# One block per layer from the output projection to the first expert gathers, with the first token tile ahead of the second

## The chip, the cores and the metric

One NeuronCore of a Trainium2 chip runs the whole program. The metric is the device time of one execution in microseconds (us), as the median of several runs. The engines of the core are PE (TensorE, matrix products; PEld is its loading of weights), DVE (VectorE), ACT (ScalarE), POOL (GpSimd) and SP (SyncE, which issues most DMAs). SBUF is the working memory, PSUM takes what PE computes.

## What is computed

Two layers of a network over 256 context and 512 latent tokens, 1024 numbers each, everything in 32-bit floats. Each layer is an attention part and a part with experts. What matters here is the end of the one and the start of the other:

```python
x = x + gate1 * (o @ w_out)                                  # output projection, gated
h = modulate(rmsnorm(x, norm2), shift, scale)                # normed, (1 + scale), + shift
q = (h @ wq).reshape(T, P_HEADS, 2, P_DKEY // 2)             # 16 half heads of 128
s = jnp.einsum("thpd,hpnd->thpn", q, sub_keys)               # scores against 128 keys each
sv, si = lax.top_k(s, P_TOPK)                                # 16 best of 128
cand = (sv[:, :, 0, :, None] + sv[:, :, 1, None, :]).reshape(T, P_HEADS, P_TOPK * P_TOPK)
fv, fi = lax.top_k(cand, P_TOPK)                             # 16 best of 256, per head
...                                                          # eidx from si and fi, gate = softmax(fv)
a = gelu(einsum("tkd,td->tk", u_tab[eidx], h)) * gate        # 128 experts for each token
x = x + gate2 * einsum("tk,tkd->td", a, v_tab[eidx])
```

The rows `u_tab[eidx]` and `v_tab[eidx]` lie in HBM side by side and are fetched by an indirect DMA, one row of 8 KB for each token and expert.

## The kernel before, in words

Tokens are cut into tiles of 128 (P): tiles 0 and 1 are the context, 2 to 5 the latent tokens. A `Stage` holds buffers and semaphores. A `Block` is a set of programs, one for each engine, with a barrier of all engines at its end; the semaphores of a stage are cleared by SP behind it. One block follows another.

In each layer two tiles are brought as far as their scores before the gathers start (tiles 0 and 1 in layer 0, tiles 2 and 3 in layer 1), and the others follow beside the gathers. Five blocks lie one behind another:

1. `turn_h` (L334): PE transposes the two tiles of attention output, ACT copies them to `m.hT`. SP issues the loads for this block and the next: the output weights in two halves of 2048 KB (L376), the gate rows and the norm's vectors. In layer 1 only columns 512 to 1023 are turned, the others lie in `m.hT` already.
2. `project` (L387): PE multiplies, chunk of 512 columns by chunk and tile by tile (L418, 64 matmul instructions in four groups of 16); DVE multiplies by the gate (L450) and POOL adds to `m.R` (L461).
3. `modulated_norm` (L272): ACT squares and sums both tiles (L294) and takes one root (L296), DVE scales and shifts (L317, L320), PE transposes (L329), ACT copies to `m.hT` (L300). SP prefetches four chunks of `p_wqk` (L1708) and stores one row of the scale.
4. `first_scores` (L1715): `p_wqk` holds for each of 16 half heads one chunk of 576 KB, its query weights and its keys. They pass through a ring of four (`pre_w`). For each, PE multiplies the chunk with both tiles at once (L1746, 256 columns), ACT copies the queries (L1771), PE multiplies them with the keys (L1755), ACT copies the scores (L1775). Chunk h is loaded when the scores of chunk h-4 are done. Behind every fourth half head DVE runs `top16` for the first tile (MAX8, FIND_INDEX8, MATCH_REPLACE8, twice) over the scores, adds up the pairs (L1792) and runs `top16` over those. The second tile's scores go to DRAM (L1736).
5. `run_experts` (L2542): 128 slots for each tile. In slot n POOL issues the gather of expert n of 128 tokens into a ring of eight (L2637, 1024 KB), DVE takes the dot product with `h` (L2734), ACT applies gelu and the gate and makes a diagonal (L2754, L2756, L2760), PE adds the weighted rows into PSUM (L2771). Before the first slot, DVE runs `choose(0, True)`, which makes the expert numbers and the gates of the first tile (L2653 to L2703), and POOL waits for it:

```python
                    if n == 0:
                        pool.wait_ge(chosen, t + 1)
```

SP's queue in this block begins with the constant `iota`, the loads of the work beside the gathers (`beside.begin`: three chunks of 512 KB of output weights and rows of 512 KB), the gate `g`, and the scores of the second tile back from DRAM (L2601, four loads of 256 KB). `choose(t)` for the next tile is spread over the slots by `ChoicePlan`. `beside` is other work on PE, ACT and DVE, laid out by slot numbers by hand: in layer 0 the attention and the scores of tiles 2 to 5 (`LatentMixer`, `NextFront`), in layer 1 those of tiles 4 and 5 (`LatentPair`).

An fp32 matmul of the program is two MATMUL instructions on PE in the profile; a transpose is one.

## Time and profile before

| | |
|---|---|
| median of 3 runs | 4538.05 us (4537.26 to 4540.35) |
| span of the profiled execution | 4536.7 us |
| median of the runs less this span | 1.35 us |
| DMA moved | 1564.87 MB, mean 345 GB/s |
| busy: PE, DVE, ACT, POOL | 83%, 57%, 38%, 38% |
| first gather issued, layer 0 and layer 1 | 555.57 and 3166.40 us |
| gathers | 1280, of 1024 KB |

The profile is of one execution. Its own time outside the span is not given apart; the runs' median lies 1.35 us above the span, and this is taken as what lies around it. Times in the rows are microseconds from the start of the span. A timeline row is start, duration, engine, line, operation, what it wrote and read, how many instructions are merged in it, and in brackets how long the engine was idle before and what ended that. Granted clock 1.00 is 2.4 GHz and 0.50 is 1.2 GHz; a window's value is a mean over both.

### The profile page before, as it was taken

The numbers are of one execution on the slowest core, as the hardware profiler recorded it, in microseconds if no ns is written. First come the engines' busy times: TensorE is split into PE (matmuls) and PEld (weight loads), VectorE is DVE, ScalarE is ACT, GpSimd is POOL, SyncE is SP. The second block draws the span as 40 slices with busy tenths as digits, with TensorE's granted clock in tenths as the row PEclk, the third lists the DMA queues.
The fourth block names the chain that finished last, engine by engine and source line by source line (L and its number), as shares of the span: only waits on it lengthen the run. The fifth ranks groups of instructions, "written<-read, shape, count | busy, mean of one in ns | idle before, by whom it ended". The sixth has DMA issues, their size and how long they took to land. (4 is left out here: it accounts for less than half of the span.)

```text
span 4536.7 us, 43969 instructions
## 1 busy us (share of the span) xinstructions
PE 3771.8 (83%) x12422; PEld 1913.6 (42%) x12422; DVE 2602.3 (57%) x5662; ACT 1740.7 (38%) x5087; POOL 1715.4 (38%) x1358
## 2 busy tenths in 40 slices
PE   6987688899899898888889967675989997877777
PEld 2443544554455454444444423545444452222222
DVE  3533587656856856755654433335775557666544
ACT  1112155444544544433333322421664433333333
POOL 0100044434434444444444422000433534556675
PEclk9988899999999999999999988798999999999999
DMA  4363499999999999999999971014999999999998
GB/s 169 113 237 147 154 420 401 420 420 420 407 420 420 410 420 419 419 420 421 418 417 420 421 310 54 4 61 150 402 377 396 422 422 416 413 421 421 419 421 357
DMA packets 251863, 1564.87 MB, mean 345 GB/s; under 512 B 30946, under 2 KB 45186, under 8 KB 80228
## 3 DMA queue, kind: packets, MB, share of 16 engines
q0 software_dynamic: 185088, 1342.36, 71.7%
q1 hardware_dynamic: 64596, 216.23, 12.5%
q10 hardware_dynamic: 1936, 3.48, 0.2%
q8 instruction: 99, 1.62, 0.1%
q14 instruction: 144, 1.18, 0.1%
HBM read 1551.50 MB, written 10.46 MB: 344 GB/s over the span
## 5 line engine op out<-in xcount | busy, mean ns | idle before, releaser
L2771 PE MATMUL ps<-ex_ring,ex_diag 128*128 128x512 f32 x5120 | 2493.9, 621 | 506.1 <-ACT ex_diag L2760 481.6
L2637 POOL DMA_INDIRECT ex_ring<-in_p_uv,ex_expert x1280 | 1650.1, 1289 | 2014.0 <-PE ps L2771 1523.6
L2734 DVE SCALAR_TENSOR_TENSOR ex_ring<-ex_ring,H 128x1024 f32<-128x1024 f32 x1280 | 1561.7, 1225 | 1170.4 <-DMA ex_ring<-in_p_uv,ex_expert 1156.0
L2771 PEld LDWEIGHTS ps<-ex_ring,ex_diag 128*128 128x128 f32 x5120 | 924.6, 194 | 1728.9 <-ACT ex_diag L2760 916.5
L2754 ACT ACTIVATE ex_act_w<-ex_dots 128x1 f32<-128x1 f32 x1280 | 258.6, 202 | 1519.6 <-DVE ex_ring L2734 1512.6
L2760 ACT ACTIVATE ex_diag<-ident_sb,ex_weight 128x128 f32<-128x128 f32 x1280 | 514.6, 402 | 92.2 <-issue 5.4
L2756 ACT ACTIVATE ex_weight<-ex_act_w,ex_gates 128x1 f32<-128x1 f32 x1280 | 377.9, 295 | 90.6 <-issue 3.1
L685 PE MATMUL ps<-win_w,hT 128*128 128x512 f32 (+1 forms) x480 | 191.9, 557 | 1.9 <-PEq L281 1.4
L1917 PEld LDWEIGHTS ps<-bs_hT,bs_w 128*128 128x128 f32 x1024 | 127.4, 196 | 33.9 <-issue 33.9
L685 PEld LDWEIGHTS ps<-win_w,hT 128*128 128x128 f32 x480 | 90.3, 191 | 106.0 <-issue 103.8
L1917 PE MATMUL ps<-bs_hT,bs_w 128*128 128x128 f32 x1024 | 127.0, 278 | 0.3 <-issue 0.3
L1746 PE MATMUL ps<-hT,pre_w 128*128 128x256 f32 x512 | 115.6, 379 | 2.7 <-PEq L281 2.7
L461 POOL TENSOR_TENSOR R<-R,pout_tmp 128x512 f32<-128x512 f32 x8 | 10.1, 1265 | 267.6 <-DVEq L452 267.6
L2754 ACT ACT_TABLE_LOAD x72 | 92.4, 1283 | 47.1 <-DVE ex_ring L2734 45.9
L2734 DVE DVE_READ_ACCUMULATOR ex_ring<-ex_ring,H 128x1 f32 x1280 | 105.9, 83 | 0.0
L1746 PEld LDWEIGHTS ps<-hT,pre_w 128*128 128x128 f32 x512 | 95.0, 190 | 15.0 <-issue 3.3
L700 ACT ACTIVATE ph_sq<-ps 128x512 f32<-128x512 f32 (+1 forms) x24 | 12.4, 517 | 160.6 <-PE ps L685 160.6
L901 PEld LDWEIGHTS ps<-KV,bs_probsT 128*128 128x128 f32 x480 | 62.9, 192 | 24.0 <-issue 24.0
L418 PE MATMUL ps<-wout_w,hT 128*128 128x512 f32 x128 | 61.7, 644 | 13.5 <-DMA wout_w<-in_o_w_out 7.3
L2042 PEld LDWEIGHTS ps<-bs_w,bs_hT 128*128 128x128 f32 x512 | 63.4, 195 | 15.8 <-issue 15.8
L730 DVE TENSOR_REDUCE ph_ss<-ph_sq 128x8 f32<-128x512 f32 (+1 forms) x24 | 14.1, 586 | 96.2 <-ACT ph_sq L700 96.2
L1917 PE MATMUL ps<-K,bs_w 128*128 128x256 f32 x256 | 66.3, 382 | 0.0
(396 smaller groups left out, 3221.6 us busy)
## 6 DMA issues: line engine op xcount, KB each, us to landing
bs_w<-in_p_wqk SPq DMA_DIRECT2D x80, 576.0 KB
ca_mod_w<-in_w_mod SPq DMA_DIRECT2D x24, 1024.0 KB, 9.1
ex_ring<-in_p_uv,ex_expert POOLq DMA_INDIRECT x1280, 14.7
pre_w<-in_p_wqk SPq DMA_DIRECT2D x32, 576.0 KB, 3.7
win_mod_w<-in_w_mod SPq DMA_DIRECT2D x16, 1024.0 KB, 4.8
bs_w<-in_e_w_out_tiles SPq DMA_DIRECT2D x32, 512.0 KB
win_w<-in_e_w_in SPq DMA_DIRECT2D x9, 1024.0 KB, 11.3
mod_mod_w<-in_w_mod SPq DMA_DIRECT2D x8, 1024.0 KB, 13.1
```

The lines of the kernel that those rows point to most:

```text
L418: mm = pe.matmul(m.ps[:, b, 0:chunk], m.hT[:, k, (t - m.h0) * P:(t - m.h0 + 1) * P], w[:, q, k, :], start=(k == 0), stop=(k == KC - 1))
L685: mm = pe.matmul(m.ps[:, u % 4, 0:halves * 256], m.hT[:, k, t * P:(t + 1) * P], pre.w[:, n % 2, 0:halves, k, :], start=(k == 0), stop=(k = ...
L901: mm = pe.matmul(self.O[:, cols], self.probsT[:, r % 2, x * P:(x + 1) * P], KV[:, self.blocks(n)[j], vals], start=(j == 0), stop=(j == las ...
L1746: mm = pe.matmul(m.ps[:, h % 2, 0:NTL * P], pre.w[:, h % RING, k * P:(k + 1) * P], m.hT[:, k, cols], start=(k == 0), stop=(k == KC - 1))
L1917: mm = pe.matmul(m.ps[:, self.q_banks[u % nq], 0:cols], w[:, j * P:(j + 1) * P], self.turned_of(self.tiles_of(u), j), start=(j == 0), stop ...
L2042: mm = pe.matmul(m.ps[:, 7, c % 4 * P:(c % 4 + 1) * P], self.hT[:, k, :], w[:, k * P:(k + 1) * P], start=(k == 0), stop=(k == KC - 1), ski ...
L2637: pool.indirect_dma_start(ring[:, r, :], None, uv_rows, bass.IndirectOffsetOnAxis(ap=expert[:, t % 2, n:n + 1], axis=0),).then_inc(landed[ ...
L2734: dve.scalar_tensor_tensor(out=ring[:, r, 0:D], in0=ring[:, r, 0:D], scalar=1.0, in1=h_of(t + t0), op0=ALU.mult, op1=ALU.mult, accum_out=d ...
L2754: act.activation(act_w[:, b:b + 1], dots[:, t % 2, n:n + 1], ACT.Gelu)
L2756: act.activation(weight[:, b:b + 1], act_w[:, b:b + 1], ACT.Copy, scale=gates[:, t % 2, n:n + 1])
L2760: act.activation(diag[:, b, :], m.ident[:, :], ACT.Copy, scale=weight[:, b:b + 1]).then_inc(diag_ready, 1)
L2771: mm = pe.matmul(mix_banks(t)[:, half, :], diag[:, b, :], ring[:, r, D + half * BANK:D + (half + 1) * BANK], start=(n == 0), stop=(n == SL ...
```

## The change

The blocks 1 to 4 of each layer and `choose(0, True)` become one block, `first_choice`. Its second argument of tiles is the same pair, but the first tile goes ahead: PE turns both, projects the first (all columns), then the second, turns the first tile's norm, computes its 16 half heads with 128 columns each, and then the second tile's. Unit u is half head u % 16 of tile u // 16. The second tile's norm is turned behind unit 8. So every chunk of `p_wqk` is loaded twice, 32 loads in place of 16. Output weights come in eight loads of 512 KB, each with a semaphore. The gate's product and sum are both on DVE, POOL has no part. DVE norms the first tile before it takes the second's sums, and behind the choice it runs `expert_numbers`, the code of `choose(0, True)` as a function; ACT's exp for it stands behind unit 26. The second tile's scores stay in SBUF, in `m.later_scores` (`m.Qc`, whose life is longer now, or rows 0 and 1 of `m.R`), where `run_experts` reads them: no store and no loads through DRAM. In `run_experts` POOL's first gather has no semaphore to wait for, and counts of `chosen`, `exped`, `weighed` and `sc_read` are lower by one. `LatentPair` gets buffers of its own for what lay in `m.R`. `modulated_norm`, still used elsewhere, squares into the place of its result instead of a scratch buffer.

```diff
--- before.py
+++ after.py
...
-                    act.activation(sq[:, :], m.R[:, t, :], ACT.Square, accum_out=ss[:, t:t + 1])
+                    act.activation(h_of(t), m.R[:, t, :], ACT.Square, accum_out=ss[:, t:t + 1])
...
+def expert_numbers(dve, m, layer, t, best, pos, at_, iota, hot, posf, part, partf, num, shift, total, shifted, chosen, exped, weighed):
...
+    dve.drain()
+    dve.sem_inc(shifted, 1)
+    dve.tensor_copy(partf, part)
+    dve.drain()
+    halves = posf.rearrange("p (h s) k -> p h s k", s=2)
+    h4 = hot.rearrange("p (h k) i -> p h k i", k=TOPK)
+    for half in range(2):
+        dve.tensor_tensor(hot, iota.unsqueeze(1).broadcast_to([P, SLOTS, TOPK]),
+                          partf[:, half, :].unsqueeze(2).broadcast_to([P, SLOTS, TOPK]), ALU.is_equal)
+        dve.drain()
+        dve.tensor_tensor(h4, h4, halves[:, :, half, :].unsqueeze(2).broadcast_to([P, PH, TOPK, TOPK]), ALU.mult)
+        dve.drain()
+        dve.tensor_reduce(num[:, half, :], hot, AX.X, ALU.add)
+        dve.drain()
+    dve.scalar_tensor_tensor(out=num[:, 0, :], in0=num[:, 0, :], scalar=float(NK), in1=num[:, 1, :], op0=ALU.mult, op1=ALU.add)
+    dve.drain()
+    dve.tensor_scalar(m.expert[:, t % 2, :], num[:, 0, :], float(layer * NK * NK), None, ALU.add)
+    dve.wait_ge(exped, 1)
...
+    dve.tensor_tensor(m.gates[:, t % 2, :].rearrange("p (h k) -> p h k", k=TOPK), shift,
+                      total.unsqueeze(2).broadcast_to([P, PH, TOPK]), ALU.mult)
...
+def first_choice(nc, m, a, layer, tiles, stream, w_out, first, src_of, h_of):
...
+    NU = 2 * NH
+    HTURN, EXP_AT = 8, 26
...
+        o_loaded, q_loaded = s.sems("o_loaded", KC), s.sems("q_loaded", RING)
...
+        def load_q(sp, u):
+            sp.dma_start(w_q[:, u % RING, :], a["p_wqk"][layer, u % NH]).then_inc(q_loaded[u % RING], 16)
...
+                for k in range(KC):
+                    sp.dma_start(w_o[:, k, :], w_out[k * P:(k + 1) * P, :]).then_inc(o_loaded[k], 16)
+                sp.dma_start(gate[:, :], rows(mods[stream:stream + 1, 2 * D:3 * D])).then_inc(gate_loaded, 16)
+                sp.dma_start(gain[:, :], rows(a["norm2"][layer:layer + 1, :])).then_inc(vec_loaded, 16)
+                sp.dma_start(scale[:, :], rows(mods[stream:stream + 1, 4 * D:5 * D])).then_inc(vec_loaded, 16)
+                sp.dma_start(shift_row[:, :], rows(mods[stream:stream + 1, 3 * D:4 * D])).then_inc(vec_loaded, 16)
+                if stream:
+                    sp.dma_start(other[:, :], mods[0:1, 4 * D:5 * D]).then_inc(vec_loaded, 16)
+                for u in range(RING):
+                    load_q(sp, u)
+                sp.dma_start(iota[:, :], rows(a["iota"])).then_inc(iota_loaded, 16)
+                sp.wait_ge(scale_ready, 1)
+                sp.dma_start(keep, (other if stream else scale)[0:1, :]).then_inc(kept, 16)
+                for u in range(RING, NU):
+                    sp.wait_ge(scored, u - RING + 1)
+                    load_q(sp, u)
+                sp.wait_ge(kept, 16)
...
+                def turn(n):
+                    for k in range(first, KC):
+                        tr = pe.transpose(m.ps[:, 2 * n + k // 4, (k % 4) * P:(k % 4 + 1) * P],
+                                          src_of(tiles[n])[:, k * P:(k + 1) * P], m.ident[:, :])
+                    tr.then_inc(o_turned, 1)
+                def out(n):
+                    order = [(k, h) for k in range(KC) for h in range(2)] if n == 0 else [(k, h) for h in range(2) for k in range(KC)]
+                    for k, h in order:
+                        if n == 0 and h == 0:
+                            pe.wait_ge(o_loaded[k], 16)
+                            if k == first:
+                                pe.wait_ge(o_copied, 1)
+                        if n == 1 and h == 0 and k == first:
+                            pe.wait_ge(o_copied, 2)
+                        mm = pe.matmul(m.ps[:, 4 + 2 * n + h, :], m.hT[:, k, cols(n)], w_o[:, k, h * BANK:(h + 1) * BANK],
+                                       start=(k == 0), stop=(k == KC - 1))
+                        if k == KC - 1:
+                            mm.then_inc(out_done, 1)
...
+                def query(u):
+                    pe.wait_ge(q_loaded[u % RING], 16 * (u // RING + 1))
+                    if u % NH == 0:
+                        pe.wait_ge(h_copied, u // NH + 1)
+                    if u >= 2:
+                        pe.wait_ge(qT_ready, u - 1)
+                    for k in range(KC):
+                        mm = pe.matmul(m.ps[:, 4 + u % 2, 0:P], w_q[:, u % RING, k * P:(k + 1) * P], m.hT[:, k, cols(u // NH)],
                                        start=(k == 0), stop=(k == KC - 1))
                     mm.then_inc(q_done, 1)
...
+                def score(u):
+                    pe.wait_ge(qT_ready, u + 1)
+                    if u < 2:
+                        pe.wait_ge(out_taken, 3)
+                    else:
+                        pe.wait_ge(taken, u - 1)
+                    pe.matmul(m.ps[:, 6 + u % 2, 0:P], qT[:, u % 2, :], w_q[:, u % RING, KC * P:(KC + 1) * P],
+                              start=True, stop=True).then_inc(scored, 1)
+                for n in range(2):
+                    turn(n)
+                for n in range(2):
+                    out(n)
+                hturn(0)
+                for u in range(NU):
+                    query(u)
+                    if u:
+                        score(u - 1)
+                    if u == HTURN:
+                        hturn(1)
+                score(NU - 1)
...
+                def copy_turned(n, sem, copied, k0):
+                    act.wait_ge(sem, n + 1)
+                    act.copy(m.hT[:, k0:KC, cols(n)],
+                             m.ps[:, 2 * n + k0 // 4:2 * n + KC // 4, :].rearrange("p b (k c) -> p (b k) c", c=P)).then_inc(copied, 1)
+                def root(n):
+                    act.wait_ge(out_taken, (1, 3)[n])
+                    act.activation(sq[:, :], m.R[:, tiles[n], :], ACT.Square, accum_out=ss[:, n:n + 1])
+                    act.drain()
+                    act.activation(ss[:, n:n + 1], ss[:, n:n + 1], ACT.Sqrt, bias=m.eps[:, :], scale=1.0 / D).then_inc(rooted, 1)
+                def query(u):
+                    act.wait_ge(q_done, u + 1)
+                    if u >= 2:
+                        act.wait_ge(scored, u - 1)
+                    act.copy(qT[:, u % 2, :], m.ps[:, 4 + u % 2, 0:P]).then_inc(qT_ready, 1)
+                def score(u):
+                    act.wait_ge(scored, u + 1)
+                    dst = sc if u < NH else later
+                    act.copy(dst[:, u % NH, :], m.ps[:, 6 + u % 2, 0:P]).then_inc(taken, 1)
+                for n in range(2):
+                    copy_turned(n, o_turned, o_copied, first)
+                root(0)
+                copy_turned(0, h_turned, h_copied, 0)
+                root(1)
+                for u in range(NU):
+                    query(u)
+                    if u:
+                        score(u - 1)
+                    if u == HTURN:
+                        copy_turned(1, h_turned, h_copied, 0)
+                    if u == EXP_AT:
+                        act.wait_ge(shifted, 1)
+                        act.activation(shift[:, :, :], shift[:, :, :], ACT.Exp).then_inc(exped, 1)
+                score(NU - 1)
 
...
             def _(dve):
+                def gated(n, c0, c1, count):
+                    mix = m.ps[:, 4 + 2 * n:6 + 2 * n, :].rearrange("p b c -> p (b c)")[:, c0:c1]
+                    dve.wait_ge(out_done, count)
+                    dve.tensor_tensor(mix, mix, gate[:, c0:c1], ALU.mult)
+                    dve.drain()
+                    dve.tensor_tensor(m.R[:, tiles[n], c0:c1], m.R[:, tiles[n], c0:c1], mix, ALU.add).then_inc(out_taken, 1)
+                def norm(n):
+                    h = h_of(tiles[n])
+                    dve.wait_ge(rooted, n + 1)
+                    dve.reciprocal(ss[:, n:n + 1], ss[:, n:n + 1])
+                    dve.drain()
+                    dve.scalar_tensor_tensor(out=h, in0=m.R[:, tiles[n], :], scalar=ss[:, n:n + 1], in1=scale[:, :],
+                                             op0=ALU.mult, op1=ALU.mult)
+                    dve.drain()
+                    dve.tensor_tensor(h, h, shift_row[:, :], ALU.add).then_inc(h_ready, 1)
+                dve.wait_ge(vec_loaded, 16 * (4 if stream else 3))
+                if stream:
+                    dve.scalar_tensor_tensor(out=other[:, :], in0=other[:, :], scalar=1.0, in1=gain[0:1, :], op0=ALU.add, op1=ALU.mult)
+                dve.scalar_tensor_tensor(out=scale[:, :], in0=scale[:, :], scalar=1.0, in1=gain[:, :], op0=ALU.add, op1=ALU.mult)
+                dve.drain()
+                dve.sem_inc(scale_ready, 1)
+                dve.wait_ge(gate_loaded, 16)
+                gated(0, 0, D, 2)
+                norm(0)
+                gated(1, 0, BANK, 3)
+                gated(1, BANK, D, 4)
+                norm(1)
                 for h in range(0, NH, 4):
                     dve.wait_ge(taken, h + 4)
                     dve.sem_inc(claimed, 1)
-                    for _ in top16(dve, range(h, h + 4), m.val, sc[:, 0], rest, m.pos):
+                    for _ in top16(dve, range(h, h + 4), m.val, sc, rest, m.pos):
                         pass
                     dve.drain()
                     pairs = m.val[:, h:h + 4, :].rearrange("p (h s) k -> p h s k", s=2)
...
+                dve.wait_ge(iota_loaded, 16)
+                expert_numbers(dve, m, layer, 0, m.best[:, :, :], m.pos[:, :, :], m.at[:, :, :], iota[:, :], hot, posf[:, :, :],
+                               part[:, :, :], partf[:, :, :], num[:, :, :], shift[:, :, :], total[:, :],
+                               shifted, chosen, exped, weighed)
...
-                act.wait_ge(sc_read, self.tiles_of(u)[0] - t0)
+                act.wait_ge(sc_read, self.tiles_of(u)[0] - t0 - 1)
...
-        self.oT, self.shift = m.R[:, 0, :].rearrange("p (k c) -> p k c", c=2 * P), m.R[:, 1, :]
+        self.oT, self.shift = s.sb("oT", [P, 4, 2 * P]), s.sb("shift_row", [P, D])[:, :]
...
-        expert, gates = s.sb("expert", [P, 2, SLOTS], U32), s.sb("gates", [P, 2, SLOTS])
+        expert, gates = m.expert, m.gates
...
-        sc, rest = s.sb("sc", [P, NH, NK]), s.sb("rest", [P, NH, NK])
+        sc, rest = m.later_scores(layer), s.sb("rest", [P, NH, NK])
...
-            return late.place is not None and late.covers(t0 + t)
+            return t == 1 or late.place is not None and late.covers(t0 + t)
...
-                    if n == 0:
-                        pool.wait_ge(chosen, t + 1)
+                    if n == 0 and t:
+                        pool.wait_ge(chosen, t)
...
-                for _ in choose(0, True):
-                    pass
...
-                shift_exp(0)
...
+        def later_scores(layer):
+            both = m.R[:, 0:CT, :] if layer else m.Qc[:, :, :]
+            return both.rearrange("p t d -> p (t d)").rearrange("p (h k) -> p h k", k=NK)
...
+            with nc.sbuf_tensor("hTc", [P, KC, CT * P], F32) as m.hT:
+                first_choice(nc, m, a, 0, CTILES, 1, a["e_w_out"], 0, lambda t: m.Qc[:, t, :], lambda t: m.H[:, t, :])
...
+                m.h0 = CT
+                first_choice(nc, m, a, 1, SOON_TILES, 0, a["o_w_out"][0], C_HEADS * C_DV // P, h_of, h_of)
```

## Rows read from the trace of the kernel before

**Rows 1.** The page's slices, DMA share in tenths and GB/s, 113.4 us each.

```profile
DMA  4363499999999999999999971014999999999998
GB/s 169 113 237 147 154 420 401 420 420 420 407 420 420 410 420 419 419 420 421 418 417 420 421 310 54 4 61 150 402 377 396 422 422 416 413 421 421 419 421 357
```

**Rows 2.** The page's group of dot products over gathered rows.

```profile
L2734 DVE SCALAR_TENSOR_TENSOR ex_ring<-ex_ring,H 128x1024 f32<-128x1024 f32 x1280 | 1561.7, 1225 | 1170.4 <-DMA ex_ring<-in_p_uv,ex_expert 1156.0
```

**Rows 3.** Windows: busy us of each engine, TensorE clock, DMA share, GB/s.

```profile
411.00:429.00 18.00, 13.14 (x24) 5.75 (x25) 0.69 (x1) 0.20 (x1) 1.27 (x1) 0.70 1.00 384
461.00:524.00 63.00, 62.72 (x320) 55.73 (x319) 29.61 (x147) 11.79 (x32) 0.00 (x0) 1.00 0.35 114
535.00:556.00 21.00, 2.94 (x8) 1.75 (x8) 16.10 (x16) 1.59 (x2) 0.43 (x1) 0.50 0.57 204
700.00:2400.00 1700.00, 1506.81 (x5313) 813.91 (x5312) 1113.95 (x2379) 781.88 (x2335) 731.91 (x609) 0.97 1.01 417
3147.00:3168.00 21.00, 0.36 (x2) 0.00 (x0) 16.11 (x16) 0.86 (x2) 1.29 (x2) 0.50 0.48 176
```

**Rows 4.** Timeline of PE, layer 0: start us, duration us, what.

```profile
415.86 16.87 PE L418 MATMUL ps<-wout_w,hT 128*128 128x512 f32 x32 [5.71 <-SPq L339]
432.99 13.97 PE L418 MATMUL ps<-wout_w,hT 128*128 128x512 f32 x32 [0.26 <-issue]
...
460.82 7.14 PE L1746 MATMUL ps<-hT,pre_w 128*128 128x256 f32 x32 [1.35 <-PEq L281]
...
471.70 0.61 PE L1755 MATMUL ps<-pre_w,es_qT 128*128 128x128 f32 x4
...
522.40 1.34 PE L1755 MATMUL ps<-pre_w,es_qT 128*128 128x128 f32 x8
```

**Rows 5.** Timeline of POOL: first gather of layer 0.

```profile
555.57 1.02 POOL L2637 DMA_INDIRECT ex_ring<-in_p_uv,ex_expert  x1 [106.49 <-DVEq L2694]
```

**Rows 6.** Timeline of POOL: first gather of layer 1.

```profile
3166.40 1.05 POOL L2637 DMA_INDIRECT ex_ring<-in_p_uv,ex_expert  x1 [106.16 <-DVEq L2694]
```

**Rows 7.** Timeline of SP's DMA queue, layer 0, output weights.

```profile
406.87 1.00 SPq L376 DMA_DIRECT2D wout_w<-in_e_w_out  x2
```

**Rows 8.** Timeline of SP's DMA queue, layer 1, output weights.

```profile
3018.97 1.01 SPq L376 DMA_DIRECT2D wout_w<-in_o_w_out  x2
```

**Rows 9.** Tile pre_w: its load instructions, and issue to landing.

```profile
L1708 SPq DMA_DIRECT2D pre_w<-in_p_wqk x32: 328/328/432, 450.2 to 3122.5; - x32
...
DMA to landing us min/median/max: 3.3/3.7/7.4
```

**Rows 10.** Timeline of ACT, layer 0, around the norm.

```profile
449.41 1.06 ACT L294 ACTIVATE n_sq<-R 128x1024 f32<-128x1024 f32 x1 [38.20 <-PEq L399]
...
459.50 1.01 ACT L300 COPY hT<-ps 128x1024 f32<-128x1024 f32 x1 [1.40 <-PE ps L329]
```

**Rows 11.** Timeline of PE beside the gathers: a query of 128 tokens.

```profile
896.36 1.95 PE L1917 MATMUL ps<-bs_hT,bs_w 128*128 128x128 f32 x16
```

**Rows 12.** Timeline of DVE, layer 0, norm, choice and expert numbers.

```profile
452.44 1.28 DVE L317 SCALAR_TENSOR_TENSOR H<-R,n_ss,v_scale 128x1024 f32<-128x1024 f32 x1
...
480.66 1.08 DVE L1679 MAX8 val<-es_sc 128x8 f32<-128x128 f32 x4 [23.14 <-ACT es_sc L1775]
...
524.29 0.87 DVE L1679 MAX8 val<-es_sc 128x8 f32<-128x128 f32 x4 [1.96 <-ACT es_sc L1775]
...
534.34 0.42 DVE L1693 FIND_INDEX8 at<-best,es_left 128x8 uint32<-128x256 f32 x1
538.21 0.29 DVE L2653 CAST ex_posf<-pos 128x256 f32<-128x256 uint32 x1 [3.45 <-DMA ex_iota<-in_iota]
...
555.37 0.29 DVE L2703 TENSOR_TENSOR ex_gates<-ex_shift,ex_total 128x128 f32<-128x128 f32 x1
```

**Rows 13.** Timeline of PE, layer 1, output projection.

```profile
3026.97 16.93 PE L418 MATMUL ps<-wout_w,hT 128*128 128x512 f32 x32 [7.27 <-DMA wout_w<-in_o_w_out]
3044.16 13.97 PE L418 MATMUL ps<-wout_w,hT 128*128 128x512 f32 x32 [0.26 <-issue]
```

197 lines of the change are left out of this document (63 added, 134 removed).

## The prediction

> **What bounds the kernel now.** I read the page's slices first. In slices 6 to 23 and from 29 on, the DMA engines are 90% busy or more and move about 420 GB/s; in slices 25 to 28 and in the first five they don't [rows 1]. These full slices are the gathers. DVE, which takes every gathered row block first, waited 1170.4 us in 1280 dot products, nearly all for the gather [rows 2]. In the stretch 700 to 2400 the DMA share is 1.01 at 417 GB/s [rows 3]. So in `run_experts` the time is bytes over rate, and two things can shorten the kernel: gathers that start earlier, or fewer bytes after their start. What lies between the end of the attention and the first gather is a serial chain in which the DMA engines have little to do: 0.35 of them is used while the scores are made (461 to 524) [rows 3].
>
> That chain in layer 0, from the timelines: the output weights are asked for at 406.87 [rows 7]; PE multiplies from 415.86 to 446.96 [rows 4]; norm, roots and turning take until 460.82, when the first query starts [rows 4, 10]; 16 half heads pass at (522.40 - 471.70)/13 = 3.90 us each, two tiles at once [rows 4]; DVE starts the choice at 480.66, waits between groups, and ends its last group at 534.76; then a new block, a wait of 3.45 us for a constant, and 17.45 us of expert numbers and gates (538.21 to 555.66) [rows 12]. The first gather goes out at 555.57 [rows 5], in layer 1 at 3166.40 [rows 6].
>
> **The change, layer 0, step by step.**
>
> *Start of the projection.* Before, PE waits for 2048 KB. Now it waits for 512 KB. The nearest row is the load of 576 KB: 3.7 us, 3.3 to 7.4 [rows 9]. 406.87 + 3.7 = 410.6, 5.3 us earlier. The other seven follow at the 384 GB/s of back-to-back loads (411 to 429) [rows 3], 1.37 us each, while PE needs 1.7 us for four matmul instructions of one chunk; so PE doesn't wait again. Bounds: 3.3, and no gain (5.3 lost) if all eight land together.
>
> *Projection.* The same 64 instructions, 31.1 us [rows 4], cold start included: to 441.7. In their second half lies all of the first tile's gate product and sum, square, root, scale and shift: four DVE passes of at most 1.28 us [rows 12] and one ACT pass of 1.06 [rows 10], with small ones about 7.5 us from 427.7 on, so 435.2. The vectors it needs are behind 4.2 MB in SP's queue, 6.3 MB in all, 16.4 us at 384 GB/s, there by about 425. That cover has 6.5 us to spare; without it the 7.5 us would be on the path.
>
> *Turn and first query.* Eight transposes take 1.0 (0.12 each, from 16 instructions of 128 columns in 1.95 us [rows 11]), the copy 1.01, and 0.31 to PE's start as between 460.51 and 460.82 [rows 4, 10]: first query at 444.1, not 460.82. The second tile's gate, root and norm are done by about 448 and its turn stands behind unit 8.
>
> *Queries.* A unit has half the columns. Half of 3.90 is 1.95; 16 query instructions of 128 columns took 1.95 with the tail of the last [rows 11], and the two of the score add 0.25, so 2.2 at most. I take 2.0. What can be late next is the ring: the load for unit u is issued when the score of u-4 is done, 2.2 us after the start of query u-3, and must land before query u, so three steps must hold 2.2 + 3.7: a step of 1.97. PE and ring are nearly equal. All 32 units and the turn: 444.1 + 64 + 1.6 = 509.7.
>
> *Choice.* Before, DVE starts 19.84 us after the first query, five steps of 3.90 and 0.34 [rows 4, 12]. Now 5 x 2.0 + 0.34: at 454.4. A group takes 10.47 (524.29 to 534.76) [rows 12], longer than four steps of 2.0, so DVE now never waits: four groups are 41.9, to 496.3. Behind it 0.15 and the 17.45 of expert numbers, without the wait for the constant: 513.9. ACT's exp stands behind unit 26, at about 499, and its input is ready at 497.5; its table load falls into PE's slack. DVE, not PE, ends the block as long as a step is under (513.9 - 444.1 - 1.6)/32 = 2.13 us.
>
> *First gather.* Across a block's end PE needed 0.31; POOL has some instructions ahead of the gather, I take 0.8 (bounds 0.3 and 2): 514.7. Gain 555.57 - 514.7 = 40.9 us.
>
> **Layer 1**, the same sum: weights asked for at 3018.97 [rows 8], PE from 3022.7 instead of 3026.97, 31.16 us [rows 13] to 3053.8; 2.4 to the first query and 70.6 more as above (10.3 + 41.9 + 0.15 + 17.45 + 0.8): 3126.8. Gain 3166.40 - 3126.8 = 39.6 us.
>
> **What is given back.** Before, the loads at the head of SP's queue in `run_experts` went through while DVE made expert numbers. In 535 to 556 the queue moved 21 x 204 = 4.28 MB, in 3147 to 3168 21 x 176 = 3.70 MB [rows 3]; four loads of 256 KB of scores, 1.05 MB, fall away. The rest, 3.24 and 2.65 MB, now stands beside gathers that already fill the engines: at 417 GB/s 7.8 and 6.3 us. POOL's gathers wait for no semaphore of theirs, only for room. Bounds: nothing, if the engines have gaps to take them, and 14.1. I take all of it, since the share there is 1.01. The stored scores were hidden under DVE and bring nothing. Moving POOL's sums to DVE is in the covered stretch. The square into the result's place is the same instruction on another address: nothing.
>
> Sum: 40.9 + 39.6 - 14.1 = 66.4 us. Span 4536.7 - 66.4 = 4470.3; with the 1.35 by which the runs' median lies above the span, 4471.6 us.
>
> **The rivals.**
>
> A. As summed, 4471.6; within 4465 to 4478 for a step of 1.95 to 2.13 and the small terms. 0.56.
>
> B. The loads at the head find gaps: half of the 14.1 is saved, 4464.6, or all, 4457.5. For it: the first gather leaves the engines idle for some us. Against: those gaps were there before as well. 0.12.
>
> C. The ring sets the pace. At 2.3 us a step the block ends 32 x 0.17 = 5.4 us later, 4482.4; at 2.6, 15 us, 4501.7. For it: PE and ring are level at 3.7 us, and landings up to 7.4 exist [rows 9]. Against: those are of four asked for at once. 0.12.
>
> D. The eight chunks land together, and PE starts as late as before: 5.3 + 4.3, 4481.2. 0.14.
>
> E. The slower side. Loads on one queue don't overlap, each pays its 3.7 us in turn. Then a step is 3.7 and the block ends at 444.1 + 118.4 + 1.6 = 564.1, 50.2 later; the eight output loads end at 406.87 + 29.6 = 436.5, the projection at 452.2, 10.5 later. Both layers: 4471.6 + 121.4 = 4593. It decides from a step of 3.17 on (the gain left in a layer is 33.2; 2.13 + 33.2/32). Against: the back-to-back loads at 384 GB/s, share 1.00 [rows 3], are 1.37 us each. 0.03. The Trainium skill, "DMA: Bandwidth & Descriptors", section Bandwidth, speaks against the change: it wants transfers of at least 1 MiB for three quarters of the peak; with the same page's 2.0 us plus bytes over 436 GB/s, paid in turn, I estimate 3.2 us for each output chunk and a step of 3.35, which gives 4563. The row above shows that 512 KB loads in a queue don't pay it in turn here.
>
> F. PE's clock drops to half in the query loop: a step of 3.9, 4585. Against: the clock is 1.00 over 461 to 524 [rows 3], and PE has no more pauses now. 0.01.
>
> Something else that takes most of the gain: 0.02.
>
> **How the numbers follow.** 4471.6 is that of A. The range 4458 to 4488 takes in A, D, all of B but its end, and C up to a step of 2.47; outside are E, F and the rest of C. Within 0.2% (9 us), which is what a measurement of this kernel tells from no change, I leave 0.01; slower 0.04 (E, F and half of the rest); faster 0.95.
>
> **What would show it.** In the changed profile: first gathers near 514.7 and, from that one shifted by the gain so far (about 33), near 3094; PE's first projection instruction 3.7 us behind the first weight load; steps of 2.0 us in the queries with PE busy throughout; no idle DVE between the four groups; DVE ending the block, some 4 us behind PE; in the first 20 us of gathers DVE waiting longer than before, by 6 to 8 us in total; the rest of `run_experts` as long as before. Wrong would be a step over 2.13, a first group that starts more than 11 us behind the first query, or an expert stage that is longer or shorter than this.

## The result, and the profile after

| | median (runs) | ratio to before | span of the profiled execution |
|---|---|---|---|
| before | 4539.2 us (4) | | 4536.7 |
| changed | 4502.1 us (4: 4486.7, 4502.0, 4502.3, 4506.1) | 0.9905 [0.9881, 0.9928] | 4485.4 |
| changed, again | 4483.2 us (6) | 0.9869 [0.9843, 0.9894] | 4475.4 |
| changed, a third time | 4484.6 us (6) | 0.9870 [0.9847, 0.9892] | 4498.0 |

The change makes the kernel faster: the ratio is 0.95% under 1 in the runs behind the result (the medians of the table are 37.1 us, 0.8%, apart) and 1.3% under 1 in two later sets. The prediction of 4471.6 us, with a range to 4488, lies below the measured 4502.1; the medians of the two later sets lie inside the range. The times of this kernel spread over 30 us from run to run. One source of that is found below, ahead of the changed code.

The timeline of PE in the changed kernel's first profile, around the block of layer 0, is the counterpart of [rows 4]:

```profile
410.97 3.65 PE L1762 MATMUL ps<-ident_sb,Qc 128*128 128x128 f32 x16 [16.37 <-PEq L475]
414.81 28.23 PE L1775 MATMUL ps<-fc_w_o,hTc 128*128 128x512 f32 x64 [0.19 <-DMA fc_w_o<-in_e_w_out]
442.88 1.04 PE L1783 MATMUL ps<-ident_sb,H 128*128 128x128 f32 x8
445.11 3.81 PE L1794 MATMUL ps<-hTc,fc_w_q 128*128 128x128 f32 x32 [1.19 <-ACT hTc L1824]
...
517.25 2.05 PE L1794 MATMUL ps<-hTc,fc_w_q 128*128 128x128 f32 x16 [0.76 <-DMA fc_w_q<-in_p_wqk]
...
521.02 2.05 PE L1794 MATMUL ps<-hTc,fc_w_q 128*128 128x128 f32 x16 [1.50 <-DMA fc_w_q<-in_p_wqk]
522.91 1.01 PE L1804 MATMUL ps<-fc_w_q,fc_qT 128*128 128x128 f32 x4
```

PE computes a unit in 2.0 us, but again and again it stands until a key chunk has landed: from the start of the first query to the start of the last it takes (521.02 - 445.11)/31 = 2.45 us a unit. The timelines of DVE, ACT and POOL show who ends the block:

```profile
457.20 0.87 DVE L1649 MAX8 val<-fc_sc 128x8 f32<-128x128 f32 x4 [7.95 <-ACT fc_sc L1842]
...
516.74 0.29 DVE L1697 TENSOR_TENSOR gates<-fc_shift,fc_total 128x128 f32<-128x128 f32 x1
```

```profile
523.96 0.27 ACT L1842 COPY Qc<-ps 128x128 f32<-128x128 f32 x1 [0.35 <-PE ps L1804]
```

```profile
525.33 1.02 POOL L2747 DMA_INDIRECT ex_ring<-in_p_uv,expert  x1 [126.52 <-issue]
...
3109.41 0.97 POOL L2747 DMA_INDIRECT ex_ring<-in_p_uv,expert  x1 [295.16 <-POOLq L1737]
```

DVE has the first tile's expert numbers and gates at 517.0. PE and ACT end the block 7 us later, with the second tile's last scores, and the first gather goes out at 525.33 where it was 555.57 [rows 5]; in layer 1 at 3109.41 where it was 3166.40 [rows 6].

Who waited for the chunks is in the view of one tile, `fc_w_q`, over this block (of an instruction: shortest, median and longest ns, then first and last start; then which engine's instructions on which tile waited for a chunk, us and times):

```profile
L1735 SPq DMA_DIRECT2D fc_w_q<-in_p_wqk x32: 327/328/1110, 418.4 to 514.4; - x32
who waited for it (us, times):
...
  PEld ps L1794: 11.5, 16
  PE ps L1794: 8.2, 11
...
DMA to landing us min/median/max: 4.0/4.9/16.0
```

A chunk now takes 4.9 us to land, where it took 3.7 [rows 9]. PEld and PE belong to one engine and wait for the same chunks, so their waits must not be added: TensorE lost about 11.5 us here. (The same view also prints one sum over both, 19.7 us in 27 waits, and the expectation for five buffers below speaks of such sums, "15 to 20".)

To compare kernels I cut each span at four points: the turn's first transpose in either layer (before: 406.51 and 3017.76) and the first gather in either layer.

| us | turn starts | turn to gather, layer 0 | gather to next turn | turn to gather, layer 1 | gather to end |
|---|---|---|---|---|---|
| before | 406.5 | 149.1 | 2462.2 | 148.6 | 1370.3 |
| changed | 411.0 | 114.4 | 2469.5 | 114.6 | 1376.0 |
| changed, again | 405.3 | 111.1 | 2469.2 | 112.8 | 1376.9 |
| changed, third | 429.6 | 110.9 | 2466.6 | 113.4 | 1377.5 |
| predicted | 406.5 | 108.2 | 2470.0 | 109.0 | 1376.6 |

The first profile against before: +4.5 - 34.7 + 7.3 - 34.0 + 5.7 = -51.2, the difference of the spans within rounding. That profile is of the fastest of the four runs, 4486.7 us; the other three took 4502.0 to 4506.1 and have no profile.

### The profile page after: what moved, and what is told of

It is laid out like the page before. It is cut to its first block and busy times, and to the rows that moved or that the text cites. A ratio compares the mean times of both kernels' runs of the same rounds, so it can differ in the third digit from the quotient of the medians.

```text
span 4485.4 us, 45108 instructions
## 1 busy us (share of the span) xinstructions
PE 3780.7 (84%) x12934; PEld 1931.3 (43%) x12934; DVE 2606.0 (58%) x5668; ACT 1746.1 (39%) x5153; POOL 1703.8 (38%) x1350
## 5 line engine op out<-in xcount | busy, mean ns | idle before, releaser
L2747 POOL DMA_INDIRECT ex_ring<-in_p_uv,expert x1280 | 1648.6, 1288 | 2239.7 <-PE ps L2876 1523.9
L2861 ACT ACTIVATE ex_weight<-ex_act_w,gates 128x1 f32<-128x1 f32 x1280 | 377.0, 295 | 91.6 <-issue 4.5
L1794 PE MATMUL ps<-hTc,fc_w_q 128*128 128x128 f32 x512 | 64.1, 279 | 9.6 <-DMA fc_w_q<-in_p_wqk 8.2
L1794 PE MATMUL ps<-hT,fc_w_q 128*128 128x128 f32 x512 | 64.4, 279 | 7.3 <-DMA fc_w_q<-in_p_wqk 5.9
L700 DVE TENSOR_REDUCE ph_ss<-ph_sq 128x8 f32<-128x512 f32 (+1 forms) x24 | 14.1, 586 | 97.0 <-ACT ph_sq L670 97.0
L1794 PEld LDWEIGHTS ps<-hTc,fc_w_q 128*128 128x128 f32 x512 | 59.6, 192 | 13.0 <-DMA fc_w_q<-in_p_wqk 11.5
L1794 PEld LDWEIGHTS ps<-hT,fc_w_q 128*128 128x128 f32 x512 | 59.5, 192 | 11.0 <-DMA fc_w_q<-in_p_wqk 9.3
```

Of the source, the lines that this page charges most:

```text
L1794: mm = pe.matmul(m.ps[:, 4 + u % 2, 0:P], w_q[:, u % RING, k * P:(k + 1) * P], m.hT[:, k, cols(u // NH)], start=(k == 0), stop=(k == KC - 1))
L2747: pool.indirect_dma_start(ring[:, r, :], None, uv_rows, bass.IndirectOffsetOnAxis(ap=expert[:, t % 2, n:n + 1], axis=0),).then_inc(landed[ ...
L2861: act.activation(weight[:, b:b + 1], act_w[:, b:b + 1], ACT.Copy, scale=gates[:, t % 2, n:n + 1])
```

## The experiments

**The changed kernel again.** Nothing is edited.

> The changed kernel unchanged, for a second profile and for the spread of its times. Theory R (the ring of four chunks paces the first choice, and how fast a chunk lands differs from run to run): the median is again about 4502 with lows near 4487; if the profiled run is one of the slow ones, the extra time against the 4486.7 run stands in the two stretches from the first query to the first gather (80.2 us in the 4486.7 run), 5 to 10 us in each, and the mean step is above 2.45 us. Theory G (the gather phases or the blocks ahead of the change make the spread): the stretch from first query to first gather is 80 us as before, and the 15 us stand between the gathers or ahead of the first block.

Measured: 4483.2 us (4476.7 to 4500.6). The profiled execution is 10 us shorter than the first one: it is 5.6 shorter ahead of the block and 5.0 in the two blocks, where PEld waited 8.6 and 7.7 us for chunks instead of 11.5 and 9.3, and 0.7 longer behind them. So the blocks do differ a little from run to run, as theory R had it, but not by the 15 us that were to be explained. R's median, about 4502 again, missed by 19 us.

> The changed kernel once more, for its median. Its four runs behind the result gave 4486.7, 4502.0, 4502.3 and 4506.1 us, six later ones 4476.7 to 4500.6 with a median of 4483.2. In every profile so far the time from one run to the next differs ahead of the first block alone: the turn starts at 403.7 to 411.0 us, or at 428.8 and 430.3 in two profiles. Theory U (a stretch at half clock between 300 and 405 us comes in some runs of any kernel here, the kernel before too, four of whose 23 runs lie 20 us above the others): a median of 4476 to 4488, one or two of the runs near 4500. Rival (this kernel falls into it more often than the others): a median over 4495, most runs near 4502.

Measured: 4484.6 us (4478.1 to 4499.3), and here the profiled execution is a long one. The stretches 300 to 405 us of the second and of the third profile, by windows:

```profile
300.00:325.00 25.00, 21.97 (x81) 6.69 (x82) 7.21 (x22) 4.96 (x19) 0.00 (x0) 0.64 1.00 414
325.00:350.00 25.00, 21.40 (x96) 8.29 (x96) 12.76 (x38) 5.32 (x20) 2.05 (x4) 0.80 0.91 366
350.00:375.00 25.00, 21.76 (x138) 10.31 (x141) 11.21 (x37) 10.11 (x36) 2.05 (x4) 1.00 0.51 188
375.00:405.00 30.00, 13.17 (x92) 6.73 (x84) 12.90 (x38) 8.94 (x26) 2.05 (x4) 0.80 0.01 3
```

```profile
300.00:325.00 25.00, 20.77 (x66) 6.45 (x66) 6.45 (x20) 3.59 (x14) 0.00 (x0) 0.50 1.00 411
325.00:350.00 25.00, 22.46 (x92) 8.02 (x91) 11.58 (x32) 5.43 (x20) 2.05 (x4) 0.71 0.84 319
350.00:375.00 25.00, 22.61 (x93) 10.50 (x92) 7.65 (x27) 6.91 (x26) 0.00 (x0) 0.63 0.57 207
375.00:405.00 30.00, 29.10 (x105) 13.47 (x108) 8.45 (x29) 7.68 (x28) 2.05 (x4) 0.51 0.10 36
```

The first block is of the second profile, the other of the third. The third number from the end is the granted clock, a share of 2.4 GHz. In the third profile it is 0.63 over 350 to 375 and 0.51, nearly all at the 1.2 GHz level, over 375 to 405, where the second has 1.00 and 0.80; PE is then busy for 29.1 of the last 30 us and the turn begins late (the second row below was read up to 432 us only and has 11 of its 16 instructions):

```profile
405.34 3.65 PE L1762 MATMUL ps<-ident_sb,Qc 128*128 128x128 f32 x16 [16.37 <-PEq L475]
```

```profile
429.63 2.58 PE L1762 MATMUL ps<-ident_sb,Qc 128*128 128x128 f32 x11 [16.36 <-PEq L475]
```

That is 24.3 us ahead of the block, in the attention that the change doesn't touch. From 300 us to the turn PE executes the same work, 407 and 408 instructions, and is busy for 78.3 us in the second profile and for 102.5 in the third, so the lower clock is all of the delay. From the turn on the third profile is 1.7 us shorter than the second (4068.4 against 4070.1). Profiles of two kernels below show the same (clocks of 0.53 and 0.50 over 375 to 405, turns at 428.8 and 430.3). The first set had three of four runs near 4502; of the twelve later ones two lie near 4500. Theory U's forecast holds; why the clock is lower in some executions no run shows.

**Eight, five and three buffers for the key chunks.**

```diff
-    NH, RING = 2 * PH, 4
+    NH, RING = 2 * PH, 8        # 5 and 3 in the other two
```

> Eight buffers for the key chunks of the first choice instead of four; the memory is there, nothing else changes. Theory R: a chunk may take up to seven steps to land, so TensorE never waits for one, the step falls from 2.45 to 2.0 to 2.1 us, VectorE ends the block, and the first gather comes 6 to 7 us earlier in each layer: a profiled time near 4474 and a median near 4475, with a spread under 5 us if the ring also makes the spread (27 us below the unchanged kernel's median). Theory T (TensorE's own work is the pace, and its waits for chunks only fill gaps that would be there anyway): step 2.35 to 2.45, the time within 3 us of the unchanged kernel. Theory G: the profiled time falls by 12 us, but the spread of 15 to 20 us stays.

> Five buffers for the key chunks instead of four. Theory R as a formula: with n buffers a load goes out after the scores that used its buffer and has n-1 steps until its queries need it, so the step is the larger of TensorE's own 2.01 us (the step with eight buffers) and (2.2 + L)/(n-1), L being the landing time of a chunk, 4.9 us in the changed kernel's trace: four buffers 2.37 to 2.45, five buffers 1.8, so TensorE sets the pace. Expected: nearly no wait for a chunk (under 3 us a layer where the changed kernel has 15 to 20), block from the start of the turn to the first gather 105 to 108 us in layer 0 (changed kernel 111 to 114, eight buffers 105.5), time within 4 us of eight buffers. Rival (landing time grows with the number of loads under way, so that depth buys little by little): the block is halfway, 108 to 110 us, and TensorE still waits 6 to 10 us a layer.

> Three buffers for the key chunks. By the formula (2.2 + L)/(n-1) with L = 4.9: a step of 3.55 us, and with L = 4.1 (loads less dense, so fewer of them held up behind a slow one) 3.15 us; 29 steps that wait give 32 to 44 us more than eight buffers in each layer: block 138 to 150 us, time 4525 to 4555, so the whole gain of the change is gone or nearly so. Rival (four buffers lose to something else than the landing, such as the issue on the load queue): the step grows by less than 0.5 us over the 2.45 of four buffers, block under 130 us.

| buffers | PEld's wait for chunks, layer 0 | landing | step | (2.2 + landing)/(n-1) | block, layers 0 and 1 | time | ratio to before |
|---|---|---|---|---|---|---|---|
| 3 | 26.8 us | 3.7 | 2.96 | 2.95 | 130.4, 133.4 | 4526.0 | 0.9975 [0.9956, 0.9993] |
| 4 (changed) | 7.8 to 11.5 | 4.6 to 4.9 | 2.33 to 2.45 | 2.27 to 2.37 | 110.9 to 114.4, 112.8 to 114.6 | 4483 to 4502 | above |
| 5 | 0 | 5.0 | 2.03 | 1.80 | 106.5, 108.1 | 4466.2 | 0.9836 [0.9813, 0.9859] |
| 8 | 0 | 5.0 | 2.03 | 1.03 | 105.5, 108.0 | 4468.9 | 0.9831 [0.9806, 0.9856] |

Landing and step are those of layer 0. The step is (start of the last query's last matmul - start of the first - 1.8)/31, from the tile view of `fc_w_q`; 1.8 us lie between the first and the last matmul of one query. With three buffers:

```profile
L1794 PE MATMUL ps<-hTc,fc_w_q x512: 275/275/377, 444.5 to 538.2; 128*128 128x128 f32 x171
...
who waited for it (us, times):
...
  PEld ps L1794: 26.8, 28
  PE ps L1794: 21.5, 28
...
DMA to landing us min/median/max: 3.2/3.7/15.1
```

With five, where no wait for a chunk is listed:

```profile
L1794 PE MATMUL ps<-hTc,fc_w_q x512: 275/275/348, 443.2 to 507.9; 128*128 128x128 f32 x171
...
its engine sat idle before it (us, times) until:
  issue: 1.4, 1
  ACT hTc L1824: 1.2, 1
  ACT fc_qT L1837: 0.3, 1
...
DMA to landing us min/median/max: 4.3/5.0/16.7
```

Within 0.08 us the step is the larger of PE's own 2.03 us (in which the second tile's turn is spread) and (2.2 + L)/(n-1), with L the landing and n the number of buffers; with four buffers it is 0.06 to 0.08 above the formula, which takes the median landing. What my expectation for three buffers missed (4525 to 4555 holds the time, 138 to 150 neither block) is that L itself depends on how close the loads follow each other: 3.7 us when they are 3 us or more apart, as with three buffers and before the change (and 3.8 in the kernel below with both tiles in one pass), 4.6 to 5.0 when they are 2.0 to 2.5 us apart. Expected for eight buffers were a median near 4475 and a spread under 5 us; the median came 6 us lower and the spread was 12.5 us, so the ring doesn't make the spread.

**Every second chunk on ScalarE's queue.** Four buffers; ACT, having waited for the unit's scores, issues the load that refills its buffer.

```diff
-                for u in range(RING, NU):
+                for u in range(RING, NU, 2):
                     sp.wait_ge(scored, u - RING + 1)
                     load_q(sp, u)
...
                     act.wait_ge(scored, u + 1)
+                    if u % 2 and u + RING < NU:
+                        load_q(act, u + RING)
```

> Four buffers as in the changed kernel, but every second chunk is loaded by ScalarE's queue instead of SyncE's. In the changed kernel a chunk takes 4.9 us to land where it took 3.7 before. Theory Q (one queue hands out the packets of its transfers one after another, so that a load waits for the one ahead of it): with two queues the landing falls to 3.7 us, (2.2 + 3.7)/3 = 1.97, the step to 2.0 to 2.1, the block in layer 0 to 105 to 108 us, the time to within 4 us of five or eight buffers. Rival S (chunks are late because some of their 128 packets are slow, or the DMA engines themselves are shared): landing and step as with one queue, 2.4 us, block 111 to 114 us.

The tile view, layer 0:

```profile
L1735 SPq DMA_DIRECT2D fc_w_q<-in_p_wqk x18: 327/328/1342, 416.5 to 510.1; - x18
L1735 ACTq DMA_DIRECT2D fc_w_q<-in_p_wqk x14: 334/334/347, 450.4 to 513.2; - x14
who waited for it (us, times):
...
  PEld ps L1794: 9.9, 12
  PE ps L1794: 7.4, 10
...
DMA to landing us min/median/max: 3.6/4.8/16.4
```

Blocks of 113.4 and 115.6 us, 4482.8 us (ratio 0.9867 [0.9844, 0.9889]): the same as with one queue. A wait behind the transfer ahead in SP's queue is not what lengthens the landing; theory Q falls. The rule of the Trainium skill, "DMA: Bandwidth & Descriptors", section "Issuing engines are not separate DMA queues", is that transfers issued by several engines run on the same 16 DMA engines and that a second issuing engine saves issue time alone. The trace agrees (4.8 us to land against 4.6 to 4.9). That leaves the engines themselves. In the changed kernel, 450 to 520 us, their share is 0.76 at 237 GB/s:

```profile
450.00:520.00 70.00, 62.58 (x523) 59.38 (x521) 55.36 (x212) 16.78 (x61) 0.00 (x0) 1.00 0.76 237
540.00:560.00 20.00, 14.16 (x24) 5.43 (x23) 11.90 (x23) 9.69 (x24) 5.77 (x5) 0.78 1.02 420
```

At the 420 GB/s per 1.02 of the second row, beside the gathers, 237 GB/s would be a share of 0.58, so the engines are busy a third longer for the same bytes than in the gathers. But that doesn't tell a late chunk from an early one: where chunks land in 3.7 us the same sum gives a quarter, before the change (0.35 at 114 GB/s [rows 3]) and with three buffers (0.57 at 189 GB/s over 445 to 535), and so it does in the second profile of the changed kernel, where they take 4.7 (0.75 at 250 GB/s over 450 to 510). What grows the landing at close spacing (some late packets, theory S, or loads that overlap on the engines) stays open.

**The second tile's chunks not loaded.**

```diff
-                for u in range(RING, NU):
+                for u in range(RING, NH):
```

and `query` waits for no load beyond those.

> The second tile's sixteen chunks are not loaded; its queries take whatever stands in the ring, so the later scores of the second tile are not those of the reference. Only the first tile's sixteen queries can still wait for a chunk. Theory R: the second sixteen steps fall to 2.0 us and the first sixteen stay at about 2.4; VectorE's choice of the first tile needs only the first sixteen, so the block ends with VectorE at about 517 in layer 0 (now 524): 6 to 7 us earlier per layer, a profiled time near 4474. Theory T: the second sixteen steps stay at 2.4 us and the time within 3 us of the unchanged kernel.

This kernel leaves out sixteen loads a layer. Its blocks take 107.5 and 108.1 us; PEld waited 3.7 us for chunks in layer 0, five times, all in the first sixteen units. 4483.8 us (4467.8 to 4495.7), profiled 4468.9. So it is not the first tile's waits that cost, because DVE's choice covers them; the second tile's do, since they push PE's end past DVE's. Theory R's 6 to 7 us a layer were right (6.9 and 6.5 against the first profile); of the six times three are 4467.8 to 4475.4 and three 4492.2 to 4495.7, so the median says little.

**Both tiles in one pass, weights loaded once.** The one block per layer stays; both tiles' norm comes first, then 16 units of 256 columns.

```diff
-    NU = 2 * NH
-    HTURN, EXP_AT = 8, 26
+    NU = NH
...
-                        mm = pe.matmul(m.ps[:, 4 + u % 2, 0:P], w_q[:, u % RING, k * P:(k + 1) * P], m.hT[:, k, cols(u // NH)],
+                        mm = pe.matmul(m.ps[:, 4 + u % 2, 0:2 * P], w_q[:, u % RING, k * P:(k + 1) * P], m.hT[:, k, both],
...
                 hturn(0)
+                hturn(1)
                 for u in range(NU):
```

> The one block per layer stays, but the weights are loaded once: each chunk serves both tiles in one pass with 256 columns, after both tiles' norm. It takes the part 'first tile ahead, weights twice' away and keeps 'one block'. From the trace of before: a step for both tiles takes 3.90 us, so the sixteen end 62.4 us after the first query, then one group of 10.65 and the expert numbers 17.45, 1.1 to the gather; the first query comes some 6.7 us later than with one tile ahead. Block 34.1 + 6.7 + 62.4 + 10.65 + 17.45 + 1.1 = 132.4 us in layer 0: one block alone takes 16.7 us off the 149.06 of before, the first tile ahead the rest (to 111 to 114, or 105.5 with eight buffers). Time 4536.7 - 2 x 16.7 + 7.0 + 6.6 = 4517. Rival (nearly all of the gain comes from joining the two blocks, with their turns, barrier and round trip of scores; the order of the tiles matters little since VectorE has 60 us to do either way): block under 120 us, time under 4495.

```profile
430.27 3.65 PE L1763 MATMUL ps<-ident_sb,Qc 128*128 128x128 f32 x16 [16.54 <-PEq L475]
...
471.82 9.47 PE L1795 MATMUL ps<-hTc,fc_w_q 128*128 128x256 f32 x32 [1.19 <-ACT hTc L1826]
481.12 0.61 PE L1806 MATMUL ps<-fc_w_q,fc_qT 128*128 128x128 f32 x4
481.56 3.62 PE L1795 MATMUL ps<-hTc,fc_w_q 128*128 128x256 f32 x16
...
535.72 1.34 PE L1806 MATMUL ps<-fc_w_q,fc_qT 128*128 128x128 f32 x8
565.34 1.23 PE L895 MATMUL ps<-KV,R 64*128 64x256 f32 x3 [28.28 <-PEq L1738]
```

4533.0 us, ratio 0.9987 [0.9971, 1.0003], where 4517 was expected; blocks of 135.9 and 138.3 us, 3.5 and 6.3 over the sum. In layer 0, 0.7 of it is the first query (41.5 us behind the turn instead of 40.8) and 1.9 the first two units, 9.7 us instead of 7.8 at a granted clock of 0.75. PE is the bound here, and DVE's last group and the expert numbers come on top of it: 28.3 us in which PE stands. So of the 35 to 38 us that the change gains in the block of layer 0, 13 come from joining the blocks, with all that came along (smaller loads of the output weights, sums on DVE, no round trip of the scores), and 22 to 25 from putting the first tile ahead. Joining alone gains 13.2 + 10.4 us and gives back 6.6 + 5.7 through the moved loads; the 11 us that are left by the profile are less by the medians, 4.6, and not told from no change. The weights loaded twice cost PE 2 x 2.0 - 3.90 = 0.1 us a chunk.

**Six more loads at the head of the gather block.**

```diff
                 load_g(1 if t0 < CT else 0)
+                for n in range(6):
+                    sp.dma_start(m.extra[layer, n], a["p_wqk"][layer, n, :, 0:D]).then_inc(extra_loaded, 16)
```

> Six extra transfers of 512 KB from and to the chip's own memory stand at the head of the load queue of each of the two gather blocks; nothing reads what they write. Theory D (from the first gather on, all sixteen DMA engines are full, and whatever is loaded beside the gathers puts the end off by its bytes over the granted rate): 3.15 MB / 417 GB/s = 7.5 us per layer, 15 us in all. Theory B (the loads find gaps between the gathers): under 3 us in all, and then the 7.3 and 5.7 us that the changed kernel gave back behind its first gathers had another source than the 3.24 and 2.65 MB of moved loads.

The load queue's timeline in layer 0, and the two gathers and turns that bound the stretch and the end:

```profile
544.61 8.95 SPq L2723 DMA_DIRECT2D extra<-in_p_wqk  x6
```

```profile
540.20 1.02 POOL L2751 DMA_INDIRECT ex_ring<-in_p_uv,expert  x1 [123.75 <-issue]
...
3132.35 0.97 POOL L2751 DMA_INDIRECT ex_ring<-in_p_uv,expert  x1 [295.33 <-POOLq L1737]
```

```profile
3019.73 1.94 PE L1762 MATMUL ps<-ident_sb,H 128*128 128x128 f32 x8 [7.05 <-PEq L1622]
```

From the gather to the next turn are 3019.7 - 540.2 = 2479.5 us (2466.6 to 2469.5 in the changed kernel), from the second gather to the end 4517.9 - 3132.4 = 1385.5 (1376.0 to 1377.5): 10 to 13 and 8 to 9.5 us for 3.15 MB, somewhat over the 7.5 of theory D. The median, 4498.6 us, is 14 to 15 us above those of the two later sets of the changed kernel, as theory D had it. Theory B falls: loads beside the first gathers find no gaps, and the 4.4 to 7.3 and 5.7 to 7.2 us that the changed kernel gives back fit the 3.24 and 2.65 MB moved there. The extra transfers also write to the chip's memory, which the moved ones don't. The ratio to before is 0.9899 [0.9874, 0.9923].

**VectorE begins after two units.** With eight buffers DVE waits 6.4 us for its first scores and then ends the block.

```diff
-                for h in range(0, NH, 4):
-                    dve.wait_ge(taken, h + 4)
+                for h, n in ((0, 2), (2, 2), (4, 4), (8, 4), (12, 4)):
+                    dve.wait_ge(taken, h + n)
```

> Eight buffers, and VectorE takes its first four heads of scores as two groups of two, so that it begins its choice after two steps instead of four. With eight buffers VectorE waits 6.4 us for its first scores and then never again: it is the bound of the block. It begins 4.0 us earlier; two groups of two cost 0.5 to 1.5 us more than one of four. Theory V (VectorE bounds the block): 2.5 to 3.5 us a layer less than with eight buffers alone, block 102 to 103 us in layer 0, time 4459 to 4461 for the profiled kind of run. Rival (the second group catches up with TensorE's scores and waits, or something else ends the block): under 1 us a layer.

> Five buffers and VectorE's first four heads as two groups of two, put together as the best version: with eight buffers the two groups took 2.1 and 2.4 us off the stretch from the first query to the first gather (71.4 and 71.7 us to 69.3 and 69.3), and five buffers were no slower than eight. Theory V: a block of 104 us and 106 us, a profiled time of 4462 with a turn at 408, and a median 2 to 5 us under that of five buffers alone (4466.2), so 4461 to 4464. Rival (five buffers are just enough while VectorE is 4 us behind and not after it starts earlier): TensorE waits for chunks again, and the block is 106 us and more.

DVE's timeline with eight buffers and pairs; the first query starts at 438.5:

```profile
445.02 0.49 DVE L1649 MAX8 val<-fc_sc 128x8 f32<-128x128 f32 x2 [2.35 <-ACT fc_sc L1842]
...
451.37 0.49 DVE L1649 MAX8 val<-fc_sc 128x8 f32<-128x128 f32 x2 [0.18 <-issue]
...
457.58 0.87 DVE L1649 MAX8 val<-fc_sc 128x8 f32<-128x128 f32 x4 [0.18 <-issue]
```

It waits 2.35 us instead of 6.4, and two groups of two take 12.6 us where one of four took 11.0. First query to first gather: 69.3 us in either layer, against 71.4 and 71.7 with eight buffers alone. That is 2.1 and 2.4 us a layer where 2.5 to 3.5 were expected. With five buffers the blocks are 103.4 and 105.7 us, as expected, and PEld waits 0.7 and 0.3 us for chunks. The medians, 4468.2 (eight) and 4467.6 (five, 4459.3 to 4483.1; 4461 to 4464 were expected), don't tell this from 4468.9 and 4466.2 without it. The profiled execution of the last, 4458.0 us, is the shortest span of all; its turn began at 405.6. Five buffers alone are what beats both kernels clearly: 1.6% under before, against 1.3% for the change as it was made, and the slowest of five runs, 4467.7 us, is faster than the fastest of the sixteen of the changed kernel, 4476.7.

## Why the prediction was wrong, step by step

Two steps failed. One is the step of the query loop, where the landing of a chunk was taken too short: 3.7 us, where 4.6 to 4.9 were measured. Against five buffers it costs 9 to 14 us in the two blocks; since other terms came out better, the stretch from the turn to the end gained 5 to 11 us less than forecast. The other is the span of before, 4536.7 us, which was carried over as if the stretch ahead of the block always took 406.5 us; I put the spread of that term at nothing and gave no reason. As far as the profiles show, it is the larger part of the miss, 20 to 26 us of 30.5.

- **Start of the projection**: right. PE began 3.5 us behind the first weight load (predicted 3.7). The 384 GB/s that I took for 512 KB loads, here and against rival E, is from a window in which the two halves of 2048 KB were landing too, so it didn't show what I said. The changed kernel does: loads of 512 and 576 KB alone moved 391 GB/s over 413 to 433.
- **Projection**: mis-sized to the good. 64 instructions in 28.2 us, not 31.1, so the first query came 34.1 us behind the turn, not 37.6. Less of it ran at the low clock: 0.96 was granted over its first 13 us, where it was 0.82 over the first 16 before.
- **Queries: the step of the block that failed.** I took 2.0 us because PE needs 2.0 (it does, 2.03 with five and eight buffers) and the ring needs three steps to hold 2.2 + 3.7, 1.97. The condition was right and is borne out by three, four and five buffers. Its 3.7 was wrong: it came from loads 3.9 us apart [rows 9], and here they are 2.33 to 2.45 apart and land after 4.6 to 4.9. I had put the ring 0.03 us below PE's 2.0; with the landing at the new spacing it is 0.27 to 0.37 above, and the step was 2.33 to 2.45.
- **Choice**: that DVE ends the block fell with the step. Its own part was right: a group takes 10.7 (predicted 10.47), expert numbers and gates ended at 517.0, 71.9 us behind the first query (predicted 69.8). With these times the bound that I gave, a step of 2.13, would be 2.20, and the step passed either. The first group came 12.1 us behind the first query in two profiles, where I had put the sign of an error at 11, and 10.6 in the third. With five or eight buffers DVE does end the block, at 105.5 to 106.5 and 108.0 to 108.1 us; predicted were 108.2 and 109.0.
- **First gather**: gains of 34.7 to 38.2 us in layer 0 (predicted 40.9) and 34.0 to 35.8 in layer 1 (39.6).
- **What is given back**: right. 11.6 to 13.6 us in three profiles against 14.1, and shown by the extra loads.
- **The rivals**: C is what happened in the blocks. It was priced at 4482.4 us for a step of 2.3; the later medians are 4483.2 and 4484.6, though the projection's gain is in them too. I gave it 0.12 and A 0.56, though nothing in the trace showed a landing at the new spacing. Against C I held that the long landings belonged to four loads asked for at once, but the landing grew for loads that are merely close as well.
- **The span of before as the base: the other step that failed.** The measured 4502.1 is 30.5 us over the forecast. The blocks and the loads account for 5 to 11 of them: 80.5 - 14.1 = 66.4 predicted, 55.8 to 61.8 measured from turn to end in the three profiles. The rest, 20 to 26 us, must lie ahead of the block if the unprofiled runs had blocks like these: there the sum was made against a profile whose turn began at 406.5, and in the third profile it began 23 us later at half clock. That the three runs of 4502.0 to 4506.1 are of that kind is an inference from the three late profiles (one of this kernel, two of its variants); they have no profile of their own. Their mean clocks, 0.950 to 0.953, fit (0.953 in the third profile, 0.956 and 0.957 in the first two), but a run of 4485.3 us in the second set has 0.953 too. My range took in neither this nor all of rival C: by C's own sum its upper end, 4488, is a step of 2.39, not the 2.47 that I wrote. If that inference holds, the later medians fall inside the range because most of those runs were not of the late kind.

## What to carry to other kernels

When a change shortens the step of a loop that is fed by a ring of loads, the landing time measured at the old spacing may be too short; ask whether the ring still holds if it grows by a third, as it did here, and spend memory on one more buffer where it is there. A second pass over the same weights, each pass with half the columns, was nearly free for TensorE here and pays as soon as it brings the work that the next stage waits for forward, but joining stages without reordering them may only move transfers to where the bandwidth is already used up. And a forecast is made against one execution: look at whether a stretch ahead of the change can come out in two ways before giving a range.

## What the runs showed of the hardware

- The landing time of a 576 KB load depends on how close the loads follow: 3.7 us at 3 to 4 us apart, 4.6 to 5.0 at 2.0 to 2.5 us apart, on one queue or two (shares of 0.35 and 0.57 in the first case, 0.74 to 0.84 in the second).
- The same program, granted the same clock up to 300 us within 0.01 (second and third profile), is then granted 0.50, 0.71, 0.63 and 0.51 over the next 105 us in one execution and 0.64, 0.80, 1.00 and 0.80 in another; PE's work there takes 24 us longer. Over all profiles of the changed kernel and its variants the turn begins at 403.7 to 411.0 us or at 428.8 to 430.3.
- Transfers of 3.15 MB from and to the chip's memory beside running gathers cost 8 to 13 us where their bytes at 417 GB/s are 7.5.
